# A hybrid decoder trunk: the first 60 microseconds with rows in groups of 128 tokens, x parts of two tiles per instruction, and low-part products last

## The chip, the cores and the metric

The kernel runs on one core of one Trainium2 chip. The metric is the device time of one execution in microseconds, lower is better. The profiler gives a second figure, the span from the first to the last recorded instruction of the core.

## What is computed

One inference step of a one-layer trunk over 2048 prompt tokens and 32 sample tokens (8 sequences of 4), 2080 tokens in all, with 1024 channels.

```
x = layer_norm(x, ln_in_g, ln_in_b)
proj = x @ w_in                       # 1024 -> 9 * 256 columns
xa, ga, xb, gb, gc, q, k, v, xp = jnp.split(proj, 9, axis=-1)
...                                   # four token mixers read proj: RG-LRU, short
...                                   # gated convolution, stick-breaking attention, pooling
out = jnp.concatenate([ya, yb, yc, yd], axis=-1) @ w_out
x = layer_norm(ALPHA * x + out, ln1_g, ln1_b)
x = layer_norm(ALPHA * x + jnp.square(jax.nn.relu(x @ w_ff1)) @ w_ff2, ln2_g, ln2_b)
```

Everything is float32. The change touches only the input layer norm and the first products of the input projection.

## The kernel before

**Blocks and tiles.** The 2080 tokens are five blocks (`NB`) of 416 tokens (`BLK`). The 1024 channels are eight tiles of 128 (`KT`), numbered k = 0 to 7. The 2304 columns of the input projection are 18 column tiles of 128, called p here in the order in which they are computed (`PORD`).

**Three products for one.** To keep float32 precision, each operand is split into a high part (rounded to the engine's fp32r format) and a low part (what is left). One block, one column tile and one channel tile cost three matmuls: w_hi·x_hi, w_hi·x_lo, w_lo·x_hi. A step is one (p, block) pair: 8 channel tiles, 24 matmuls of 416 columns into one PSUM bank. `P_STEPS` lists the steps: first the four column tiles p = 0 to 3 (`GRP`) for block 0, then for block 1, and so on to block 4; then the other column tiles. The text calls step j `project(j)`.

**The input layer norm.** Block b's rows come from memory with the tokens on the partitions, 104 tokens (`ROW`) in each of four groups (`NR`), each in two pieces of 96 and 8 rows (`ROW_PARTS`). They go to `rows_a` for even b and `rows_b` for odd b. VectorE (DVE) takes statistics (`block_var`: eight `bn_stats`, four `bn_aggr`, one add), ScalarE (ACT) takes the root (`block_std`), DVE the reciprocal (`block_nmr`), and then both engines normalise the rows in place: ACT group 0 and half of group 2, DVE the rest. TensorE (PE) transposes every channel tile back to channels-on-partitions (`turn_back(b, k)`: four transposes into PSUM bank 4 + k % 4). `block_back` finishes it: ACT (even k) or DVE (odd k) applies the layer norm's gain and bias while it moves the tile from PSUM to `x_full`; ACT makes x_hi by a copy; DVE makes x_lo by a subtraction. Every x tile goes through both engines.

**The weights.** `load_raw(p)` brings one column tile (128 x 1024 floats) into one of the two slots of `w_raw`. ACT makes the high part (`split_hi(p)`), DVE the low part (`split_lo(p)`); for p = 1 alone GpSimd (POOL) makes the low part.

**Order.** Each engine runs its own instructions in the order in which they are written, and waits on semaphores. Block 0's steps for p = 0 and 1 are computed together (`project_two`), so that each x tile is used as soon as it is there. ACT also copies each finished step out of PSUM (`put_out`). All these loads and stores are issued by SyncE (SP) on one queue, in program order. After block 4's first four column tiles (about 115 us) no line of the program differs any more.

Of the kernel before, what the change touches and what calls it, by code (L numbers as in the profile page):

```python
# [15 lines left out]
P = 128  # L16
# [62 lines left out]
ROW_PARTS = ((0, 96), (96, ROW))  # L79
NATB = NR * NB  # L80
# [167 lines left out]
def build(nc, x_all, w_all, pvec, lnp, rows2, gates_a, gates_x, poolw, sbh, sbr, masks, ident_d, ck, cv, ptab,  # L248
          st_h, st_a, st_b, st_p, y_out, kv_out, so_out):
    ctx = ExitStack()  # L250
    with ctx:
# [69 lines left out]
        with ExitStack() as e1:  # L321
            sb_at("x2_and_x3", [P, 2, 2, KT, BLK], F32, X_AT, e1)
# [103 lines left out]

        def raw_halves(n):

            return raw[:, n % 2, :].rearrange("p (k h c) -> p h k c", h=2, c=P)
# [8 lines left out]
        s_raw = [sem("raw_in0"), sem("raw_in1")]  # L438
        s_wh, s_wl = sem("w_hi_made"), sem("w_lo_made")
# [121 lines left out]
        def _(sp):  # L561
# [36 lines left out]
            load_rows(0)  # L598
            const(ident[:, :], ident_d)
# [238 lines left out]
        def _(pe):  # L838
            def turn_back(b, k):
# [6 lines left out]
                for j in range(NR):  # L846
                    ins = pe.transpose(PS[:, 4 + k % 4, j * ROW:(j + 1) * ROW], x_rows(b)[0:ROW, j, k * P:(k + 1) * P],
                                       ident[0:ROW, 0:ROW])
# [25 lines left out]
            def project_two():  # L874

                for k in range(KT):
                    pe.wait_ge(s_xl, k + 1)
                    for p in range(2):
                        if k == 0:
                            pe.wait_ge(s_wl, p + 1)  # L880
                        w_h, w_l = w_at(wp_hi(p), k), w_at(wp_lo(p), k)
                        out = PS[:, p, 0:BLK]
# [1716 lines left out]
```

## Time and profile before

| quantity | value |
|---|---|
| median of 3 executions | 2454.24 us (2453.53 to 2456.04) |
| profiled execution: its own time | 2453.47 us |
| profiled execution: span | 2451.9 us |
| TensorE matmul busy | 2410.5 us (98%) |
| VectorE busy | 1587.5 us (65%) |
| ScalarE busy | 1287.9 us (53%) |
| GpSimd busy | 242.4 us (10%) |

The profiled execution's own time lies 1.57 us above its span and 0.77 us below the median of the three. Busy time is time in which an engine works on an instruction; the idle time before an instruction is put down to whatever released it last. TensorE's matmuls are pipelined, so one matmul's printed duration (0.35 us) is longer than the distance from its start to the next one's (0.19 us): throughput is read from the starts.

### The profile page before, as it was taken

How to read it: one execution, taken by the hardware profiler on the slowest of the kernel's cores; microseconds unless marked ns; L12 is line 12 of the kernel's file. 1: busy time of each engine (PE TensorE's matmuls, PEld its weight loads, DVE VectorE, ACT ScalarE, POOL GpSimd, SP SyncE). 2: the span in 40 equal slices, each digit the busy share in tenths (PEclk: the TensorE clock that was granted, in tenths of full speed). 3: DMA queues.
4: the chain of work that ended last, by engine and by line, in shares of the span. 5: the costliest groups of instructions: out<-in, count | busy, mean ns of one | idle time of the engine just before them, and what ended most of it. 6: DMA issues, size and time to landing. Idle time of an engine off the chain costs nothing.

```text
span 2451.9 us, 36722 instructions
## 1 busy us (share of the span) xinstructions
PE 2410.5 (98%) x13263; PEld 2330.7 (95%) x13263; DVE 1587.5 (65%) x2234; ACT 1287.9 (53%) x1981; POOL 242.4 (10%) x526
## 2 busy tenths in 40 slices
PE   7999999999999999999999999999999999999998
PEld 7999999999999999999999999999999999999998
DVE  7535662656777787777778777757755665863335
ACT  5466523545656745556555566554445555444432
POOL 0011320200101100111100011000122130000000
PEclk9999999999999999999999999999999999999999
DMA  8434554533444434444443443433566674343332
GB/s 256 152 110 140 165 170 131 168 120 127 160 126 157 130 117 140 131 149 141 122 131 124 130 146 115 133 115 117 173 192 183 203 238 140 117 136 120 112 115 86
DMA packets 141526, 351.64 MB, mean 143 GB/s; under 512 B 20625, under 2 KB 64146, under 8 KB 141218
## 3 DMA queue, kind: packets, MB, share of 16 engines
q1 hardware_dynamic: 128994, 312.88, 40.2%
q0 software_dynamic: 12352, 36.42, 4.7%
q8 instruction: 106, 1.74, 0.3%
q14 instruction: 74, 0.61, 0.1%
HBM read 300.11 MB, written 49.12 MB: 142 GB/s over the span
## 4 chain that ended last, share of the span: by engine, by line
PE 92%; DVE 3%; ACT 2%; issue 1%; DMA 1%; SPq 0%; DVEq 0%; ACTq 0%
PE PS L1133 21%; PE PS L1135 21%; PE PS L1134 21%; PE PS L871 5%; PE PS L869 5%; PE PS L870 5%; PE PS L939 2%; PE PS L961 1%; PE PS L960 1%; PE PS L929 1%; PE PS L1023 1%; PE PS L930 1%; PE PS L1053 1%; PE PS L1011 1%; PE PS L909 1%
## 5 line engine op out<-in xcount | busy, mean ns | idle before, releaser
L1433 ACT ACTIVATE w_hi_lo<-w_raw 128x1024 fp32r<-128x1024 f32 x240 | 253.0, 1054 | 282.8 <-PE PS L1135 276.7
L1133 PE MATMUL PS<-a_hi,w_hi_lo 128*128 128x416 f32 x1080 | 385.0, 356 | 1.9 <-DVE a_lo L2185 1.9
L1135 PE MATMUL PS<-a_hi,w_hi_lo 128*128 128x416 f32 x1080 | 378.9, 351 | 0.0
L1134 PE MATMUL PS<-a_lo,w_hi_lo 128*128 128x416 f32 x1080 | 378.1, 350 | 0.0
L1986 DVE TENSOR_TENSOR w_hi_lo<-w_raw,w_hi_lo 128x1024 fp32r<-128x1024 f32 x240 | 292.7, 1220 | 57.2 <-ACT w_hi_lo L1433 54.9
L1133 PE MATMUL PS<-h_hi,w_hi_lo 128*128 128x416 f32 x824 | 294.3, 357 | 0.0
L1135 PE MATMUL PS<-h_hi,w_hi_lo 128*128 128x416 f32 x824 | 289.8, 352 | 0.0
L1134 PE MATMUL PS<-h_lo,w_hi_lo 128*128 128x416 f32 x824 | 288.9, 351 | 0.0
L2013 DVE TENSOR_TENSOR h_lo<-h_full,h_hi 128x416 fp32r<-128x416 f32 x160 | 94.6, 592 | 224.1 <-ACT h_hi L1448 223.9
L1133 PEld LDWEIGHTS PS<-a_hi,w_hi_lo 128*128 128x128 f32 x1080 | 202.8, 188 | 5.4 <-DVE a_lo L2185 2.8
L1134 PEld LDWEIGHTS PS<-a_lo,w_hi_lo 128*128 128x128 f32 x1080 | 203.3, 188 | 2.1
L1135 PEld LDWEIGHTS PS<-a_hi,w_hi_lo 128*128 128x128 f32 x1080 | 202.4, 187 | 2.3
L1433 ACT ACTIVATE w_hi_lo_c<-w_raw 128x1024 fp32r<-128x1024 f32 x120 | 126.5, 1054 | 132.8 <-PE PS L1135 128.4
L1444 ACT ACTIVATE h_full<-PS 128x416 f32<-128x416 f32 x160 | 82.5, 516 | 200.6 <-PE PS L1135 198.8
L1133 PE MATMUL PS<-a_hi,w_hi_lo_c 128*128 128x416 f32 x520 | 185.2, 356 | 2.2 <-DVE a_lo L2019 2.0
L1942 DVE TENSOR_TENSOR_SCAN n_prompt<-n_prompt 128x512 f32<-128x512 f32 (+3 forms) x160 | 178.9, 1118 | 8.6 <-POOL n_prompt L2508 8.4
L1135 PE MATMUL PS<-a_hi,w_hi_lo_c 128*128 128x416 f32 x520 | 183.2, 352 | 0.0
L1134 PE MATMUL PS<-a_lo,w_hi_lo_c 128*128 128x416 f32 x520 | 182.5, 351 | 0.0
L1986 DVE TENSOR_TENSOR w_hi_lo_c<-w_raw,w_hi_lo_c 128x1024 fp32r<-128x1024 f32 x120 | 146.3, 1220 | 34.1 <-ACT w_hi_lo_c L1433 33.2
L1134 PEld LDWEIGHTS PS<-h_lo,w_hi_lo 128*128 128x128 f32 x824 | 155.6, 189 | 2.1
L1133 PEld LDWEIGHTS PS<-h_hi,w_hi_lo 128*128 128x128 f32 x824 | 155.3, 188 | 2.2 <-issue 0.4
L1135 PEld LDWEIGHTS PS<-h_hi,w_hi_lo 128*128 128x128 f32 x824 | 154.8, 188 | 1.6
(334 smaller groups left out, 5206.4 us busy)
## 6 DMA issues: line engine op xcount, KB each, us to landing
w_raw<-w_all SPq DMA_DIRECT2D x380, 512.0 KB, 3.5
proj_scratch<-stage SPq DMA_DIRECT2D x70, 208.0 KB, 2.0
k_rows<-kv_out SPq DMA_DIRECT2D x80, 128.0 KB, 4.1
v_hi_lo<-v_scratch SPq DMA_DIRECT2D x40, 256.0 KB, 4.3
x_scratch<-x_full SPq DMA_DIRECT2D x20, 416.0 KB, 2.7
x_residual<-x_scratch SPq DMA_DIRECT2D x5, 1664.0 KB, 7.8
pages<-ck SPq DMA_DIRECT2D x64, 128.0 KB, 2.2
pages<-ck POOLq DMA_DIRECT2D x64, 128.0 KB, 2.6
```

What stands on the lines that cost most here:

```text
L869: pe.matmul(out, w_h, x_hi(b)[:, k, :], start=(k == 0), stop=False)
L870: pe.matmul(out, w_h, x_lo(b)[:, k, :], start=False, stop=False)
L871: ins = pe.matmul(out, w_l, x_hi(b)[:, k, :], start=False, stop=(k == KT - 1))
L939: ins = pe.transpose(PS[:, 5 + 2 * (t % 2), j * P:(j + 1) * P], sP[:, t % 3, j * P:(j + 1) * P], ident[:, :])
L1133: pe.matmul(out, w_h, mh_[:, k, :], start=(g == 0), stop=False)
L1134: pe.matmul(out, w_h, ml_[:, k, :], start=False, stop=False)
L1135: ins = pe.matmul(out, w_l, mh_[:, k, :], start=False, stop=(g == KT - 1))
L1433: act.activation(halves(w_hi(n)), raw_halves(n), ACT.Copy).then_inc(s_wh, 1)
L1444: act.activation(hf[:, f % 2, :], PS[:, (N_P + n) % 3, 0:BLK], ACT.Relu).then_inc(s_r, 1)
L1942: dve.tensor_tensor_scan(rev(n_t[:, 0:w]), rev(n_t[:, 0:w]), rev(n_t[:, 0:w]), n_t[:, w:w + 1], ALU.mult, ALU.bypass).then_inc(s_scan2, 1)
L1986: dve.tensor_tensor(halves(w_lo(n)), raw_halves(n), halves(w_hi(n)).bitcast(F32), ALU.subtract).then_inc(s_wl, 1)
L2013: dve.tensor_tensor(hl[:, i, :], hf[:, f % 2, :], hh[:, i, :].bitcast(F32), ALU.subtract).then_inc(s_hl, 1)
```

## The change

- **Rows.** A block's 416 tokens are cut into groups of 128, 128, 128 and 32 (`GROUPS`), each loaded by one transfer. SP waits until the second group of block 0 has landed before it issues anything else. The number of statistics, normalising and transpose instructions stays the same; their partition counts and widths change. `mv` is set to 1.0 beforehand, because the last group fills only 32 partitions.
- **Raw weights 2 and 3** get places of their own (in the idle tile `x2_and_x3`, called `x_and_x` in the rows), so their loads wait for nothing.
- **x parts.** ACT makes x_hi, and DVE x_lo, for two channel tiles (128 x 832) in one instruction. Each engine fills `x_full` for the next pair before it makes the parts of this pair.
- **Weight low parts.** DVE makes the low part for p = 1 too (POOL no longer), and `split_lo(0)`, `(1)`, `(2)` stand behind block 0's x parts. `split_hi(1)` stands behind x_hi of the first pair.
- **project_two** issues the two products with w_hi for all k first; the 16 products with w_lo follow as a group.
- **PE.** Four float32 matmuls on zeros stand ahead of everything (they wait for the second row group). `turn_back(1, 0..3)` moves from ahead of `project(3)` into its middle, `turn_back(1, 4..7)` from its middle to its end.

```diff
             def load_raw(p):
-                if p >= 2:
-                    sp.wait_ge(s_wl, p - 1)
+                if p in (2, 3):
+                    spare = x23[:, 1, p - 2, :, :].rearrange("p k t -> p (k t)")
+                    sp.dma_start(spare[:, 0:KT * P], w_all[AT[PORD[p]]]).then_inc(s_raw2[p - 2], 16)
+                    return
+                if p >= 4:
+                    sp.wait_ge(s_wl, p - 3 if p < 6 else p - 1)
...
-                for j in range(NR):
-                    at = b * BLK + j * ROW
-                    for first, last in ROW_PARTS:
-                        sp.dma_start(x_rows(b)[first:last, j, :], x_all[at + first:at + last]).then_inc(
-                            s_xin[b % 2] if b else s_xr0[j], 16)
+                for j, (first, last) in enumerate(GROUPS):
+                    sp.dma_start(x_rows(b)[0:last - first, j, :], x_all[b * BLK + first:b * BLK + last]).then_inc(
+                        s_xin[b % 2] if b else s_xr0[j], 16)
...
             load_rows(0)
+            sp.wait_ge(s_xr0[1], 16)
             const(ident[:, :], ident_d)
             const(ln_gb[:, :, :], lnp)
             load_raw(0)
             load_raw(1)
             load_rows(1)
             load_raw(2)
+            load_raw(3)
             for k in range(0, KT, 2):
                 store_x1(0, k)
-            load_raw(3)
...
                     for p in range(2):
                         if k == 0:
-                            pe.wait_ge(s_wl, p + 1)
+                            pe.wait_ge(s_wh, p + 1)
...
-                        ins = pe.matmul(out, w_l, x_hi(0)[:, k, :], start=False, stop=(k == KT - 1))
-                        if k == KT - 1:
-                            ins.then_inc(s_pst, 1)
-
+                for p in range(2):
+                    pe.wait_ge(s_wl, p + 1)
+                    for k in range(KT):
+                        ins = pe.matmul(PS[:, p, 0:BLK], w_at(wp_lo(p), k), x_hi(0)[:, k, :], start=False, stop=(k == KT - 1))
+                    ins.then_inc(s_pst, 1)
+
+            pe.wait_ge(s_zero, 1)
+            pe.wait_ge(s_xr0[1], 16)
+            for _ in range(4):
+                pe.matmul(PS[:, 7, 0:BLK], x23[:, 0, 0, 0, 0:P], x23[:, 0, 0, 0, :], start=True, stop=True)
...
+                    if b or p >= 2:
+                        project(b * GRP + p, turned=range(4) if b == 0 and p == 3 else ())
                     if b == 0 and p == 3:
-                        for k in range(4):
+                        for k in range(4, KT):
                             turn_back(1, k)
-                    if b or p >= 2:
-                        project(b * GRP + p, turned=range(4, KT) if b == 0 and p == 3 else ())
...
             def block_back(b, ks):                      # ACT
-                for k in ks:
-                    if k % 2 == 0:
...
-                    act.activation(x_hi(b)[:, k, :], x_full(b, k), ACT.Copy).then_inc(s_xh, 1)
+                whole(ks[0])
+                for k in ks[::2]:
+                    if k + 2 in ks:
+                        whole(k + 2)
+                    wait_apart(act, s_xfa, b * 4 + k // 2 + 1)
+                    act.wait_ge(s_xfd, b * 4 + k // 2 + 1)
+                    act.activation(x_hi(b)[:, k:k + 2, :], x_full(b, k, 2), ACT.Copy).then_inc(s_xh, 2)
+                    if b == 0 and k == 0:
+                        split_hi(1)
...
             def block_back(b, ks):                      # DVE
...
+                whole(ks[0] + 1)
+                for k in ks[::2]:
+                    if k + 2 in ks:
+                        whole(k + 3)
+                    dve.wait_ge(s_xh, b * KT + k + 2)
+                    dve.tensor_tensor(x_lo(b)[:, k:k + 2, :], x_full(b, k, 2), x_hi(b)[:, k:k + 2, :].bitcast(F32),
+                                      ALU.subtract).then_inc(s_xl, 2)
...
             dve.memset(gsel[:, :, :, :], 0.0).then_inc(s_mzero, 1)
+            dve.memset(x23[:, 0, 0, 0, :], 0.0).then_inc(s_zero, 1)
+            own.up(dve.memset(mv[:, :, :], 1.0))
             block_var(0)
             block_nmr(0)
-            split_lo(0)
             dve.wait_ge(s_const, 32)
             block_back(0, range(KT))
-            dve.wait_ge(s_wl, 2)
-            split_lo(2)
+            for p in range(3):
+                split_lo(p)
             block_var(1)
+            split_lo(3)
             block_nmr(1)
-            split_lo(3)
...
         def _(pool):
-            pool.wait_ge(s_wl, 1)
-            pool.wait_ge(s_wh, 2)
-            pool.tensor_tensor(halves(wp_lo(1)), raw_halves(1), halves(wp_hi(1)).bitcast(F32), ALU.subtract).then_inc(s_wl, 1)
```

DVE's instructions of the change's core, before: from the normalising of block 0's rows to the end of `split_lo(3)`. The left word is the line, then the operation, the written tile, the read tiles and the shape.

```order
L1722 TENSOR_SCALAR rows_a<-rows_a,rstd,nmr 104x1024 [waits nmr_made]
...
L1687 TENSOR_TENSOR w_hi_lo<-w_raw,w_hi_lo 128x2x512 [waits w_hi_made]
L1730 TENSOR_SCALAR x_full<-PS,ln_gb 128x416 [waits back_transposed,const_in]
L1734 TENSOR_TENSOR x_early<-x_full,x_early 128x416 [waits x_hi_made] x2
...
L1687 TENSOR_TENSOR w_hi_lo<-w_raw,w_hi_lo 128x2x512 [waits w_hi_made,w_lo_made]
L1697 BN_STATS bn<-rows_b 104x6 [waits xin_in_b]
L1697 BN_STATS bn<-rows_b 104x6 x7
...
L1722 TENSOR_SCALAR rows_b<-rows_b,rstd,nmr 104x1024
L1687 TENSOR_TENSOR w_hi_lo<-w_raw,w_hi_lo 128x2x512 [waits w_hi_made]
L1730 TENSOR_SCALAR x_full<-PS,ln_gb 128x416 [waits x_hi_made,x1_stored0,back_transposed]
```

The same stretch of DVE after the change:

```order
L1769 TENSOR_SCALAR x_full<-PS,ln_gb 128x416 [waits back_transposed,const_in]
L1769 TENSOR_SCALAR x_full<-PS,ln_gb 128x416 [waits back_transposed]
L1777 TENSOR_TENSOR x_early<-x_full,x_early 128x832 [waits x_hi_made]
...
L1777 TENSOR_TENSOR x_early<-x_full,x_early 128x832 [waits x_hi_made] x2
L1719 TENSOR_TENSOR w_hi_lo<-w_raw,w_hi_lo 128x2x512 [waits w_hi_made] x2
L1719 TENSOR_TENSOR w_hi_lo<-x_and_x,w_hi_lo 128x2x512 [waits w_hi_made]
L1733 BN_STATS bn<-rows_b 128x6 [waits xin_in_b]
L1733 BN_STATS bn<-rows_b 128x6 x5
L1733 BN_STATS bn<-rows_b 32x6 x2
...
L1719 TENSOR_TENSOR w_hi_lo<-x_and_x,w_hi_lo 128x2x512 [waits w_hi_made]
L1751 RECIPROCAL rstd<-std 128x4 [waits tile_normalised,std_made]
```

The first weight split has left its place ahead of block 0's x parts, three splits stand behind them, the fourth stands ahead of block 1's normalising instead of behind it, and eight single x_lo instructions have become four of 832 columns.

PE's instructions around the end of block 0, before (each row of L869 to L871 stands for one of 24 matmuls of a step):

```order
L871 MATMUL PS<-x_early,w_hi_lo 128x416
L847 MATMUL PS<-ident,rows_b 128x104 x16
L869 MATMUL PS<-x_early,w_hi_lo 128x416
...
L871 MATMUL PS<-x_early,w_hi_lo 128x416
L847 MATMUL PS<-ident,rows_b 128x104 x16
L869 MATMUL PS<-x_early,w_hi_lo 128x416
```

and after:

```order
L888 MATMUL PS<-x_early,w_hi_lo 128x416
L865 MATMUL PS<-ident,rows_b 128x128 x3
L865 MATMUL PS<-ident,rows_b 128x32
...
L886 MATMUL PS<-x_early,w_hi_lo 128x416
L887 MATMUL PS<-x_early,w_hi_lo 128x416
L888 MATMUL PS<-x_early,w_hi_lo 128x416
```

Before, the first 16 transposes of block 1 stand behind `project(2)` and the second 16 behind the first 12 matmuls of `project(3)`; after, the first 16 stand behind 36 matmuls (`project(2)` and half of `project(3)`) and the second 16 behind 12 more.

## Rows read from the trace of the kernel before

**Rows 1.** The page: busy us, share of the span and instructions of each engine.

```profile
PE 2410.5 (98%) x13263; PEld 2330.7 (95%) x13263; DVE 1587.5 (65%) x2234; ACT 1287.9 (53%) x1981; POOL 242.4 (10%) x526
```

**Rows 2.** A stage: us, busy PE, PEld, DVE, ACT, POOL, clock, DMA share, GB/s.

```profile
60.00:70.00 10.00, 10.00 (x63) 9.89 (x62) 8.32 (x14) 4.32 (x8) 0.00 (x0) 1.00 0.78 210
```

**Rows 3.** Timeline of PE: start us, us, line, what, count, idle before.

```profile
15.56 5.09 PE L847 MATMUL PS<-ident,rows_a 104*128 104x104 f32 x28 [15.56 <-ACT rows_a L1286]
21.73 0.96 PE L847 MATMUL PS<-ident,rows_a 104*128 104x104 f32 x4 [1.08 <-DVE x_full L1730]
...
22.88 0.55 PE L884 MATMUL PS<-x_early,w_hi_lo 128*128 128x416 f32 x1
...
24.96 0.45 PE L884 MATMUL PS<-x_early,w_hi_lo 128*128 128x416 f32 x1
25.25 0.35 PE L885 MATMUL PS<-x_early,w_hi_lo 128*128 128x416 f32 x1
...
32.78 0.35 PE L869 MATMUL PS<-x_early,w_hi_lo 128*128 128x416 f32 x1
...
37.31 1.59 PE L847 MATMUL PS<-ident,rows_b 104*128 104x104 f32 x16
38.68 0.43 PE L869 MATMUL PS<-x_early,w_hi_lo 128*128 128x416 f32 x1
...
54.30 1.62 PE L847 MATMUL PS<-ident,rows_a 104*128 104x104 f32 x16 [0.34 <-ACT rows_a L1286]
...
135.50 1.56 PE L909 MATMUL PS<-a_conv,gsel 128*128 128x416 f32 x4
```

**Rows 4.** Timeline of DVE, with the same columns.

```profile
4.77 1.29 DVE L1697 BATCH_NORM_STATS2 bn<-rows_a 104x6 f32<-104x512 f32 x2 [2.91 <-DMA rows_a<-x_all]
...
10.57 1.29 DVE L1697 BATCH_NORM_STATS2 bn<-rows_a 104x6 f32<-104x512 f32 x2 [0.26 <-DMA rows_a<-x_all]
...
13.43 1.99 DVE L1722 TENSOR_SCALAR rows_a<-rows_a,rstd,nmr 104x1024 f32<-104x1024 f32 x3
16.41 1.23 DVE L1687 TENSOR_TENSOR w_hi_lo<-w_raw,w_hi_lo 128x1024 fp32r<-128x1024 f32 x1 [0.99 <-ACT w_hi_lo L1271]
17.55 0.70 DVE L1730 TENSOR_SCALAR x_full<-PS,ln_gb 128x416 f32<-128x416 f32 x1
18.59 2.47 DVE L1734 TENSOR_TENSOR x_early<-x_full,x_early 128x416 fp32r<-128x416 f32 x2 [0.33 <-ACT x_early L1299]
...
23.52 1.20 DVE L1734 TENSOR_TENSOR x_early<-x_full,x_early 128x416 fp32r<-128x416 f32 x2
...
28.13 4.84 DVE L1697 BATCH_NORM_STATS2 bn<-rows_b 104x6 f32<-104x512 f32 x8
...
45.81 4.84 DVE L1697 BATCH_NORM_STATS2 bn<-rows_a 104x6 f32<-104x512 f32 x8
...
51.73 0.18 DVE L1715 RECIPROCAL rstd<-std 104x4 f32<-104x4 f32 x1 [0.27 <-ACT std L1279]
...
52.21 1.99 DVE L1722 TENSOR_SCALAR rows_a<-rows_a,rstd,nmr 104x1024 f32<-104x1024 f32 x3
```

**Rows 5.** Groups of one shape, 12 to 56 us: busy us, mean ns.

```profile
L1299 ACT ACTIVATE x_early<-x_full 128x416 fp32r<-128x416 f32 x16 | 8.6, 551 | 2.5 <-DVE x_full L1730 1.5
...
L1294 ACT ACTIVATE x_full<-PS,ln_gb 128x416 f32<-128x416 f32 x9 | 6.2, 687 | 0.3 <-PE PS L847 0.3
...
L1271 ACT ACTIVATE w_hi_lo<-w_raw 128x1024 fp32r<-128x1024 f32 x4 | 4.1, 1045 | 0.0
...
L2409 POOL TENSOR_TENSOR w_hi_lo<-w_raw,w_hi_lo 128x1024 fp32r<-128x1024 f32 x1 | 2.4, 2382 | 17.1 <-DVE w_hi_lo L1687 17.1
```

**Rows 6.** Single microseconds of the transfers: us, clock, DMA share, GB/s.

```profile
10.00:11.00 1.00, 1.00 1.02 387
11.00:12.00 1.00, 1.00 1.04 406
12.00:13.00 1.00, 1.00 1.06 246
```

More of the change, by code:

```diff
@@ L79 @@
 ROW_PARTS = ((0, 96), (96, ROW))
+GROUPS = [(a, min(a + P, BLK)) for a in range(0, BLK, P)]
 NATB = NR * NB
@@ L425, in halves, with raw_at, raw_in_halves @@
             return bass.AP(w[0], w[1] * HALF, [[WT, P], [ODD, 2], [P, KT // 2], [1, P]])
+        def raw_at(n):
+            return raw[:, n % 2, :]
+        def raw_in_halves(p):
+            if p not in (2, 3):
+                return raw_halves(p)
+            spare = x23[:, 1, p - 2, :, :].rearrange("p k t -> p (k t)")
+            return spare[:, 0:KT * P].rearrange("p (k h c) -> p h k c", h=2, c=P)
         def raw_halves(n):
-            return raw[:, n % 2, :].rearrange("p (k h c) -> p h k c", h=2, c=P)
+            return raw_at(n).rearrange("p (k h c) -> p h k c", h=2, c=P)
         def w_at(w, k):
@@ L845, in turn_back @@
                     pe.wait_ge(s_xfd if k % 2 else s_xfa, b * 4 + (k - 4) // 2 + 1)
-                for j in range(NR):
-                    ins = pe.transpose(PS[:, 4 + k % 4, j * ROW:(j + 1) * ROW], x_rows(b)[0:ROW, j, k * P:(k + 1) * P],
-                                       ident[0:ROW, 0:ROW])
+                for j, (first, last) in enumerate(GROUPS):
+                    n = last - first
+                    ins = pe.transpose(PS[:, 4 + k % 4, first:last], x_rows(b)[0:n, j, k * P:(k + 1) * P], ident[0:n, 0:n])
                 ins.then_inc(s_bt, 1)
@@ L1264, in split_hi @@
             def split_hi(p):
-                act.wait_ge(s_raw[p % 2], 16 * (p // 2 + 1))
+                if p in (2, 3):
+                    act.wait_ge(s_raw2[p - 2], 16)
+                else:
+                    act.wait_ge(s_raw[p % 2], 16 * max(p // 2, 1))
                 if p >= 4:
@@ L1278, in block_std @@
                 act.wait_ge(s_ve, b + 1)
-                act.activation(std[0:ROW, :], var[0:ROW, :], ACT.Sqrt).then_inc(s_std, 1)
+                act.activation(std[:, :], var[:, :], ACT.Sqrt).then_inc(s_std, 1)
             def block_norm(b):
@@ L1714, in block_nmr @@
                     dve.wait_ge(s_nat, NR * b)
-                own.up(dve.reciprocal(rstd[0:ROW, :], std[0:ROW, :]))
+                own.up(dve.reciprocal(rstd[:, :], std[:, :]))
                 own.sync()
-                dve.scalar_tensor_tensor(out=nmr[0:ROW, :], in0=mv[0:ROW, :, 0], scalar=-1.0, in1=rstd[0:ROW, :], op0=ALU.mult,
+                dve.scalar_tensor_tensor(out=nmr[:, :], in0=mv[:, :, 0], scalar=-1.0, in1=rstd[:, :], op0=ALU.mult,
                                          op1=ALU.mult).then_inc(s_nmr, 1)
@@ L1720, in block_nmr, with whole @@
                 for j, start in ((1, 0), (2, D // 2), (3, 0)):
-                    row = x_rows(b)[0:ROW, j, start:D]
-                    dve.tensor_scalar(row, row, rstd[0:ROW, j:j + 1], nmr[0:ROW, j:j + 1], ALU.mult, ALU.add).then_inc(s_natv, 1)
+                    row = x_rows(b)[0:size(j), j, start:D]
+                    dve.tensor_scalar(row, row, rstd[0:size(j), j:j + 1], nmr[0:size(j), j:j + 1], ALU.mult,
+                                      ALU.add).then_inc(s_natv, 1)
             def block_back(b, ks):
-                for k in ks:
-                    if k % 2:
-                        dve.wait_ge(s_bt, b * KT + k + 1)
-                        place_free(dve, s_xh, b, k)
-                        dve.tensor_scalar(x_full(b, k), PS[:, 4 + k % 4, 0:BLK], ln_gb[:, 0, k:k + 1], ln_gb[:, 1, k:k + 1],
-                                          ALU.mult, ALU.add).then_inc(s_xfd, 1)
-                        for d in (k - 1, k):
-                            dve.wait_ge(s_xh, b * KT + d + 1)
-                            dve.tensor_tensor(x_lo(b)[:, d, :], x_full(b, d), x_hi(b)[:, d, :].bitcast(F32), ALU.subtract).then_inc(s_xl, 1)
+                def whole(k):
+                    dve.wait_ge(s_bt, b * KT + k + 1)
+                    place_free(dve, s_xh, b, k)
+                    if b == NB - 1 and k >= 4:
+                        dve.wait_ge(s_xl, b * KT + k - 3)
+                    dve.tensor_scalar(x_full(b, k), PS[:, 4 + k % 4, 0:BLK], ln_gb[:, 0, k:k + 1], ln_gb[:, 1, k:k + 1],
+                                      ALU.mult, ALU.add).then_inc(s_xfd, 1)
```

47 lines of the change are left out of this document (25 added, 22 removed).

## The prediction, made before the changed kernel ran

> **What bounds the kernel now.** I read the busy time by engine first: PE is busy in 2410.5 of 2451.9 us [rows 1]. The stages then show where it is not: from 60 us on it is busy in 10.00 of 10 [rows 2], and the lines of the change end at about 115 us. So only the start can give something, and a microsecond won there is a microsecond of the whole, if nothing takes it back. The timeline of PE shows what there is to win [rows 3]: PE waits until 15.56 us for block 0's normalised rows, again 1.08 us before the last four transposes, and once more at 54.30 us for block 2's rows (0.34 us by the row). A 416-column matmul follows the one before at 0.35 us between 22.88 and 24.96 (six in 2.08 us: 1.2 GHz), and at 0.188 us from 25.25 to 32.78 (40 of them: the 2.4 GHz level). The granted clock in the stage rows says 1.00 throughout, so here I trust the starts.
>
> The timeline of DVE shows who makes PE wait [rows 4]. The row groups land one after another, the first at 4.77 and the last at 10.57 us, and everything up to 15.42 us (13.43 + 1.99) is a chain behind the last one. From 37 us to 54.20 us DVE works almost without a pause, and its normalising of block 2 (52.21 + 1.99 = 54.20) is what PE waits for at 54.30. **That is the point I calculate to**: from block 2's transposes on, PE has no further wait, so the kernel ends earlier by what those transposes start earlier than 54.30. PE may be far ahead in between; it must wait there for DVE.
>
> **Rows in 128-token groups.** The transfer rate is 246 GB/s while rows go (12 to 13 us), and 387 and 406 GB/s while the two raw weight tiles pass (10 to 12 us, mean 396) [rows 6]. Those have 128 partitions of 4 KB, exactly the form of the new groups; the rows before go in pieces of 96 and 8. At 396 GB/s a group of 524 KB takes 1.3 us, against 426 KB at 246 GB/s, 1.7 us. The first lands at 4.77 - 0.4 = 4.4 us, the next at 5.7, 7.0 and (32 rows) 7.4. Two statistics instructions take 1.2 us (8 in 4.84 [rows 4]), so DVE hardly waits: the third pair starts at 7.05 and all is done 2.45 later, at 9.5 us, against 10.57 + 1.29 = 11.86. **Gain 2.35 us**, and block 0's normalising ends at 13.1 us instead of 15.42. Holding back the later loads costs nothing: raw weight 0 is issued near 7 us and needed at 13.1, which covers more than twice its own 1.3 us; the two memsets on DVE (the nearest row, 128x768 zeros, is not longer than DVE's 2.91 us wait for the first rows) lie ahead of the first rows.
>
> By the Trainium skill (page "DMA: Bandwidth & Descriptors", section "Why a DMA increments its semaphore by 16 and not by 1") a transfer uses the largest number of engines, at most 16, that divides its partition count: 96 partitions run on 16 engines, 8 on 8. By that rule the busiest engine has 7 rows of an old group and 8 of a new one, and the old form would not be slow; the rate in the rows says that it is. This is a rival below.
>
> **DVE's chain from there, step by step.** Starts of neighbours lie a little closer than their durations, so I use distances between starts. Prices: x_full 0.70 (0.65 to the next), weight low part 1.15 (16.41 to 17.55), statistics up to the variance 5.6 (45.81 to 51.46, where the 0.27 us of waiting for the root begin), reciprocal to the end of normalising 2.47 (51.73 to 54.20) [rows 4]. ACT: x_full 0.69, weight high part 1.0 [rows 5]. The pair of 832 columns is in no row. It lies between 416 and 1024 columns: on ACT 0.55 and 1.05, on DVE 0.60 (half of 1.20) and 1.23 [rows 4, 5]; by the length I take 0.9 and 1.02. The bounds, 1.05 and 1.23 per pair above and half of that below, move a block by at most 0.8 us. One tile's four transposes take 0.343 us at the upper level (16 in 1.37, 37.31 to 38.68), 0.73 at the lower one (28 in 5.09) [rows 3].
>
> *PE's clock.* The four float32 matmuls on zeros start near 5.7. Four of that shape take 1.56 us at the upper level [rows 3] (L909, 135.50), so about 3 at the lower one: they end near 8.8, and PE idles until 13.2. Before, 28 transposes in 5.09 us did not raise the clock, so I take the lower level for block 0's transposes, and the upper one some us later, as before.
>
> *Block 0.* Transposes from 13.2: tile 1 is there at 14.9 and tile 3 at 16.3. x_full of 1 ends at 15.6, of 3 at 17.0. ACT has done weight 0 (14.0), x_full of 0 and, behind tile 2, of 2 (16.3), and the first x_hi pair at 17.1. x_lo pair and x_full of 5 to 18.8; wait 0.75, since ACT puts the high part of weight 1 in between (pair 2 at 19.5). Three more x_lo pairs with x_full of 7: 23.1. Three weight low parts, 3.45: 26.6.
> *Block 1's rows.* Statistics 5.6: 32.2. Weight 3, 1.15: 33.35. Reciprocal to normalised, 2.47: 35.8. PE transposes at 35.9 (before 37.31).
> *Block 1's x.* x_full of 1 and 3 until 38.2, first pair of x_hi at 38.8, x_lo pair until 39.8. Then a new wait: tiles 4 and 5 are transposed only behind four tiles (1.37) and 12 matmuls (2.26), from 39.55, and are there at 40.5. x_full of 5, x_hi pair at 41.7, three pairs of x_lo with x_full of 7: 45.25.
> *Block 2.* From the statistics' start to the transposes 8.49 (45.81 to 54.30): **53.7 us instead of 54.30, a gain of 0.6 us**.
>
> So the way from block 0's rows to block 2's is 1.7 us longer than before (40.5 against 38.8), though two things on it get cheaper. POOL's weight low part (2.38 us [rows 5]) is gone, beside which two x_lo instructions took 2.47 instead of 1.20 us [rows 4]: 1.27 saved. Four pairs instead of eight singles save 4 x 0.18 us in each of the blocks 0 and 1, together 1.4. Against that stand 1.15 for the fourth weight low part on DVE, the waits of 0.75 and 0.7 above, 0.5 to 0.6 at each first pair, that the first x_full pair now waits for transposes at the lower level (about 1.0; before, a weight split filled that time), and that the last weight part now stands ahead of block 1's normalising (1.15, of which 0.8 had been waited anyway).
>
> **PE's part.** project_two can begin near 18.8; its 48 matmuls, 9.0 us at 0.188 and about 1 us more at first, end near 29, some 4 us before the 32.78 of before. But that lead is given back by waits behind it: for the fourth weight low part (33.4) before project(3), for x_lo in block 1's first step, and about 2.7 us before block 2's transposes. Issuing the w_lo products last is therefore worth nothing at the end, and the zero matmuls, which lie in a wait, cost nothing.
>
> **The sum.** Span 2451.9 - 0.6 = 2451.3, the profiled execution 2453.47 - 0.6 = 2452.9. The median of the runs lies 0.77 above that execution: 2454.24 - 0.6 = **2453.6 us**. 0.2% of the time, about what a measurement can tell from no change, is 4.9 us.
>
> **Rivals.**
> 1. *The rows come no faster.* The 246 GB/s belong to the source, not to the form. Then a group takes 2.1 us: landings at 5.2, 7.3 and 9.3, statistics done at 11.75 (gain 0.1 instead of 2.35), and with the 1.7 from above the kernel is **1.6 us slower**. Against it stand the 387 and 406 of [rows 6], seen with the same partitions and row length. The skill's rule above gives nearly this: 8/7 of the mean landing distance ((10.57 - 4.77)/3 = 1.93) is 2.2 us. Chance 0.18.
> 2. *The clock is up from block 0 on.* The zero matmuls raise it and it stays up. A tile's transposes then take 0.343 instead of 0.73, x_full of 1 starts at 14.1 and all behind it is 1.0 earlier: **gain 1.6 us**. Against it, 5.09 us of transposes did not raise it, and the zeros are shorter and followed by 4.4 us of nothing. Chance 0.16.
> 3. *The other side: the clock falls in the new wait.* PE now waits some 2.7 us before block 2's transposes, where it waited 0.34. A way back from the low level is in the rows: 21.73 to 24.96 us, four transposes at +0.09 each and eight matmuls at +0.16, 1.6 us lost [rows 3]; the whole low stretch from 15.56 would be 4.7 us. With one such return the kernel is 1.0, with the long one **4.1 us slower**; it turns slower once the low stretch exceeds 1.2 us. For it speaks that PE was at the low level at 22 us after a pause of 1.08; against it, that PE had then never been at the upper one. Chance 0.10. The Trainium skill (page "TensorE: Matmul & The Clock Gate", section "HAM oscillation") says that matmul bursts with long waits between them fall back to half rate each time.
> 4. *The lead is kept.* If DVE's chain is shorter than I have it (pairs near the lower bound, no waits), PE keeps its 4 us or more: **gain 3 to 5.6 us**. Against it: DVE has 39 us of work in a row there. Chance 0.08.
>
> **How the numbers follow.** The forecast has 0.43 (0.2 slower to 1.3 faster), the rivals 0.52, the rest 0.05. The number is the forecast's, 2453.6. The range leaves out the far parts of rivals 3 and 4 (each by half) and little else: gain 4.2 to 2.6 slower, 2450.0 to 2456.8, which also takes in that three executions of one kernel lay 2.5 us apart. Faster by over 4.9 us is only the far end of rival 4: 0.03. Slower by as much needs rivals 1 and 3 at once: 0.02. Within 0.2%: 0.95.
>
> **What would show it.** Row landings: the second pair of statistics follows the first with hardly a wait, the last ends near 9.5. Chain: block 0's transposes near 13.2, project(2) near 29, project(3) waiting for the fourth weight low part until 33.4, block 2's transposes near 53.7 with an idle time of about 2.7 before them, none behind 60 us. Clock: transposes of one tile 0.73 apart at 13 us, 0.35 between matmuls at first, 0.188 soon after. Wrong would be: statistics still paced by landings; tiles 0.34 apart at 13 us; 0.35 between matmuls behind 53 us; or no wait at all before block 2.

## The result and the profile after

| | before | after |
|---|---|---|
| median | 2453.91 us (2453.53 to 2456.04) | 2471.14 us (2470.61 to 2473.34, 4 executions) |
| ratio after to before | | 1.0069, 95% interval 1.0057 to 1.0082 |
| profiled execution, span | 2453.47, 2451.9 us | 2471.05, 2469.3 us |

The kernel is 17 us slower, and the interval leaves no room for no change. The page's first row, as in [rows 1], shows on which engine: PE is busy 22.7 us longer with eight more records, while DVE and ACT have hardly changed. So PE's own instructions take longer.

```profile
PE 2433.2 (99%) x13271; PEld 2340.4 (95%) x13271; DVE 1584.8 (64%) x2217; ACT 1285.4 (52%) x1961; POOL 243.5 (10%) x525
```

The timeline of PE after, the counterpart of [rows 3] (start us, us, line, what, count, idle before):

```profile
5.98 4.88 PE L910 MATMUL PS<-x_and_x 128*128 128x416 f32 x8 [5.98 <-DMA rows_a<-x_all]
14.02 8.63 PE L865 MATMUL PS<-ident,rows_a 128*128 128x128 f32 x32 [3.16 <-ACT rows_a L1311]
22.58 0.71 PE L899 MATMUL PS<-x_early,w_hi_lo 128*128 128x416 f32 x1
...
30.63 3.19 PE L904 MATMUL PS<-x_early,w_hi_lo 128*128 128x416 f32 x16
...
40.48 2.62 PE L865 MATMUL PS<-ident,rows_b 128*128 128x128 f32 x16
43.03 0.46 PE L886 MATMUL PS<-x_early,w_hi_lo 128*128 128x416 f32 x1
...
86.23 2.62 PE L865 MATMUL PS<-ident,rows_b 128*128 128x128 f32 x16
88.78 0.46 PE L886 MATMUL PS<-x_late,w_hi_lo 128*128 128x416 f32 x1
...
151.21 1.56 PE L931 MATMUL PS<-a_conv,gsel 128*128 128x416 f32 x4
```

Sixteen transposes in a row are four tiles; the text calls them a burst. Before, a burst took 1.37 us up to the next matmul (37.31 to 38.68 in [rows 3]); now it takes 2.55 (86.23 to 88.78), though PE waits for no other engine there. That is 0.30 us more per tile, at every one of the 24 tiles of blocks 2 to 4, where each microsecond of PE counts. The last row is the first matmul of the later gates (L909 in [rows 3]). It comes at 151.21 instead of 135.50 us, 15.7 later, and what follows it takes 2318.1 us against 2316.4, which is within the 2316 to 2320 of the other traces. **I call this start the gate mark below.** The only two traces of one kernel (E7 and E14) had it at 134.20 and 134.69. Executions of one kernel lie 2.5 us and more apart in the whole time, so the mark seems the sharper measure, though each kernel has it from one trace.

PE's weight loads at 86 us name the place inside a tile:

```profile
86.04 0.44 PEld L865 LDWEIGHTS PS<-ident,rows_b 128*128 128x128 f32 x3
86.64 0.48 PEld L865 LDWEIGHTS PS<-ident,rows_b 32*128 32x128 f32 x4 [0.17 <-issue]
87.30 0.48 PEld L865 LDWEIGHTS PS<-ident,rows_b 32*128 32x128 f32 x4 [0.17 <-issue]
```

Each row of four is one 32-row load and the three 128-row loads of the next tile, 0.65 us from row to row. Before each 32-row load the loader stands still for 0.17 us though the profile shows nothing that it awaits (`issue`). Before the change all 16 loads stand in one row without idle time:

```profile
37.12 1.57 PEld L847 LDWEIGHTS PS<-ident,rows_b 104*128 104x128 f32 x16
```

DVE after, the counterpart of [rows 4]:

```profile
4.66 2.50 DVE L1733 BATCH_NORM_STATS2 bn<-rows_a 128x6 f32<-128x512 f32 x4 [2.33 <-DMA rows_a<-x_all]
7.88 2.46 DVE L1733 BATCH_NORM_STATS2 bn<-rows_a 128x6 f32<-128x512 f32 x4 [0.72 <-DMA rows_a<-x_all]
...
11.89 1.98 DVE L1758 TENSOR_SCALAR rows_a<-rows_a,rstd,nmr 128x1024 f32<-128x1024 f32 x3
16.32 0.71 DVE L1769 TENSOR_SCALAR x_full<-PS,ln_gb 128x416 f32<-128x416 f32 x1 [2.44 <-PE PS L865]
18.39 0.71 DVE L1769 TENSOR_SCALAR x_full<-PS,ln_gb 128x416 f32<-128x416 f32 x1 [1.36 <-PE PS L865]
...
41.84 0.71 DVE L1769 TENSOR_SCALAR x_full<-PS,ln_gb 128x416 f32<-128x416 f32 x1 [3.90 <-PE PS L865]
...
57.74 1.98 DVE L1758 TENSOR_SCALAR rows_a<-rows_a,rstd,nmr 128x1024 f32<-128x1024 f32 x3
```

The rows do land sooner: statistics end at 10.34 (7.88 + 2.46), not at 11.86. But now DVE waits for PE's transposes (2.44, 1.36, 3.90 us), and block 2's normalising ends at 59.72 (57.74 + 1.98) instead of 54.20. The stages (us, busy PE, PEld, DVE, ACT, POOL, clock, DMA share, GB/s) add the clock:

```profile
12.00:14.00 2.00, 0.00 (x0) 0.01 (x1) 1.87 (x3) 2.00 (x3) 0.00 (x0) 0.78 1.00 410
14.00:26.00 12.00, 11.98 (x42) 8.69 (x43) 7.22 (x9) 9.34 (x12) 0.00 (x0) 0.50 0.78 277
...
56.00:60.00 4.00, 1.65 (x10) 1.31 (x9) 3.10 (x11) 2.41 (x4) 0.00 (x0) 1.00 0.70 255
60.00:62.00 2.00, 2.00 (x11) 1.23 (x10) 0.71 (x1) 0.84 (x2) 0.00 (x0) 0.73 0.31 111
62.00:66.00 4.00, 4.00 (x14) 3.42 (x14) 1.64 (x2) 2.38 (x3) 0.00 (x0) 0.50 0.51 197
```

The granted clock is at 0.50 (1.2 GHz) in block 0, and again from 61 to 67 us, behind the wait ahead of block 2 (PE busy 1.65 of 4 us).

### The profile page after: what moved, and what is told of

It reads as the page before. It is cut to its first block, busy times and chain, and to the rows that moved or that the text cites. A ratio compares the mean times of both kernels' runs of the same rounds, so it can differ in the third digit from the quotient of the medians.

```text
span 2469.3 us, 36723 instructions
## 1 busy us (share of the span) xinstructions
PE 2433.2 (99%) x13271; PEld 2340.4 (95%) x13271; DVE 1584.8 (64%) x2217; ACT 1285.4 (52%) x1961; POOL 243.5 (10%) x525
## 4 chain that ended last, share of the span: by engine, by line
PE 93%; DVE 3%; ACT 2%; issue 1%; DMA 0%; DVEq 0%; ACTq 0%; SPq 0%
PE PS L1155 21%; PE PS L1157 21%; PE PS L1156 21%; PE PS L886 5%; PE PS L888 5%; PE PS L887 5%; PE PS L961 2%; PE PS L983 1%; PE PS L982 1%; PE PS L951 1%; PE PS L1045 1%; PE PS L952 1%; PE PS L1075 1%; PE PS L1033 1%; PE PS L865 1%
```

## The experiments

"Theory A" in the expectations is that the step in height (the rows of the weight) between a 128-row and a 32-row transpose costs 0.30 us per tile. All kernels compute the whole of the reference. Where no other kernel is named, ratios are to the kernel before, run on the same chip in the same turn.

**E1: the kernel before, with the changed groups alone.**

```diff
+GROUPS = [(a, min(a + P, BLK)) for a in range(0, BLK, P)]   # 128, 128, 128, 32
...
-                for j in range(NR):
-                    ins = pe.transpose(PS[:, 4 + k % 4, j * ROW:(j + 1) * ROW], x_rows(b)[0:ROW, j, k * P:(k + 1) * P],
-                                       ident[0:ROW, 0:ROW])
+                for j, (first, last) in enumerate(GROUPS):
+                    n = last - first
+                    ins = pe.transpose(PS[:, 4 + k % 4, first:last], x_rows(b)[0:n, j, k * P:(k + 1) * P], ident[0:n, 0:n])
```

> The kernel before with one part of the change alone: rows in groups of 128, 128, 128 and 32 tokens. Theory A (the step between a 128-row and a 32-row weight in PE's transposes costs time): a tile's four transposes start 0.65 us after the last tile's instead of 0.34, 40 tiles give 12 us, so 2463 to 2468 us. Theory B (the loss comes from the moved waits and the clock they cost, and a tile is slow only where PE waits): within 2 us of 2454, tiles 0.34 to 0.36 us apart. Theory C (any transpose of 128 rows and columns is slow): as A, but the time lies in the 128-row ones, which would start 0.18 us apart.

Measured: 2464.71 us, ratio 1.0041 (1.0026 to 1.0055), gate mark 146.12: as theory A had it. The groups alone cost 10.6 us at the gate mark, although block 0's transposes begin at 14.34, 1.2 us sooner than before. Block 2's begin 3.4 us later (57.70 against 54.30), and six bursts of 1.2 us more are the rest. The burst at 81 us:

```profile
81.14 2.62 PE L847 MATMUL PS<-ident,rows_b 128*128 128x128 f32 x16
83.69 0.46 PE L868 MATMUL PS<-x_late,w_hi_lo 128*128 128x416 f32 x1
```

**E2: the changed kernel with four groups of 104 again**, each one transfer.

```diff
-GROUPS = [(a, min(a + P, BLK)) for a in range(0, BLK, P)]
+GROUPS = [(a, a + ROW) for a in range(0, BLK, ROW)]
```

> The changed kernel with four groups of 104 rows again, each in one transfer. Theory A: all tiles 0.34 us apart, the wait before block 2 is back to under 2 us, 2451 to 2456 us. Theory B: the reordered waits remain, so 2464 to 2470 us.

**E3: the changed kernel, its last transpose made over 128 rows**, of which 96 are zeros.

```diff
-                    n = last - first
+                    n, last = P, first + P
...
+            for t in (rows_a, rows_b):
+                pool.memset(t[:, NR - 1, :], 0.0).then_inc(s_pad, 1)
```

> The changed kernel with the last group's transposes made 128 rows tall and 128 columns wide (96 of the rows are zeros that are written once at the start, their columns are not read). Theory A: no step in height is left, a tile takes 0.44 us (512 columns in two passes), 40 x 0.21 = 8.4 us and some of the follow-up are won, 2457 to 2463 us. Theory C: 128-row transposes are slow themselves, a tile takes 0.7 us or more, 2472 us or more. Theory B: no difference from the changed kernel, 2470 to 2472 us.

Measured: E2 2458.40 us, ratio 1.0016 (1.0006 to 1.0025), gate mark 137.67; E3 2457.40 us, 1.0012 (1.0003 to 1.0022), gate mark 138.27. Taking the 32-row transposes away, in two ways, takes 13.5 and 12.9 us of the 15.7 off. E3 keeps the count of transposes and the quick transfers and even transposes more columns, so neither the count nor the bytes cost. Theory A had E2 at 2451 to 2456 us, so it was missed by 2.4: some 2 to 3 us are left. In E2 they are a late start, block 2's transposes beginning at 56.46 instead of 54.30. In E3 those begin at 53.69, 0.6 sooner than before; its padded bursts cost 0.3 each (6.28 from one to the next where it was 5.98 before), 1.8 in six; and block 2's two bursts are 7.86 apart and not 6.28, 1.6 us. Together these give 138.3, the mark that E3 has. The last part is the clock, in single microseconds around block 2's start:

```profile
53.00:54.00 1.00, 0.31 (x2) 0.34 (x3) 0.59 (x1) 1.00 (x2) 0.00 (x0) 0.72 0.00 0
54.00:55.00 1.00, 1.00 (x7) 1.00 (x6) 0.00 (x0) 0.20 (x2) 0.00 (x0) 0.50 0.22 60
```

In block 0, however, E3's clock stayed up, unlike the changed kernel's, and 32 transposes took 3.69 us:

```profile
13.51 3.69 PE L868 MATMUL PS<-ident,rows_a 128*128 128x128 f32 x32 [3.01 <-ACT rows_a L1314]
```

```profile
14.00:16.00 2.00, 2.00 (x21) 2.00 (x20) 1.23 (x2) 1.89 (x4) 0.00 (x0) 1.00 1.08 383
```

**E4: E2 with block 1's `turn_back` where it was before the change.**

```diff
-                        project(b * GRP + p, turned=range(4) if b == 0 and p == 3 else ())
                     if b == 0 and p == 3:
-                        for k in range(4, KT):
+                        for k in range(4):
                             turn_back(1, k)
+                    if b or p >= 2:
+                        project(b * GRP + p, turned=range(4, KT) if b == 0 and p == 3 else ())
```

> As the one with 104-row groups, and block 1's transposes back in their old places (four tiles ahead of project(3), four in its middle). My ledger has 0.7 us of DVE waiting for tiles 4 and 5 and, on the other side, PE waiting for block 1's rows ahead of project(3): 0 to 1.5 us faster than with the new places. Rival: the new places keep PE dense, and the old ones cost 1 us or more.

Measured: 2459.32 us, 1.0021 (1.0011 to 1.0030), gate mark 141.44. With the old places PE waits for block 1's rows instead, 2.85 us, and the clock falls there:

```profile
39.40 3.01 PE L865 MATMUL PS<-ident,rows_b 104*128 104x104 f32 x16 [2.85 <-ACT rows_b L1311]
```

The mark is 3.8 us later than E2's, so the rival of the expectation came out and not the 0 to 1.5 us gain. The new places of `turn_back` are therefore no cost of the change; whether they gain is not told by the whole times, whose intervals overlap.

**E5 and E6: the fourth group as a plain float32 matmul over 128 rows**, of 32 columns, in the changed kernel (E5) and the kernel before with the new groups (E6).

```diff
+                    ins = pe.matmul(PS[:, 4 + k % 4, first:last], x_rows(b)[:, j, k * P:(k + 1) * P], ident[:, 0:last - first],
+                                    start=True, stop=True, is_transpose=True if j < NR - 1 else None)
```

> The changed kernel with all weights of the transposes 128 rows tall and the old 416 columns: the last group's rows 32 to 127 are zeros written once, and its 32 columns come from a plain float32 matmul with the identity's first 32 columns. Theory A (the step in height costs the time): tiles 0.35 us apart, 2.9 us less than with the padded 512 columns, block 2's transposes near 53.5: 2453.5 to 2456 us. Rival (any change between neighbours costs, the change from transpose to plain matmul as well): tiles 0.5 us or more, 2457 to 2462 us.

> The kernel before with the 128-token row groups and the same even heights, nothing else of the change. Theory A: tiles 0.35 us apart. The transposes of block 0 start near 14.3, 1.2 us earlier than before, but before block 2 PE is held by its own work (it waited 0.34 there), so 0 to 0.8 us faster than before: 2453.5 to 2454.5 us. Rival (the 128-token groups bring 1.2 us or more by themselves): under 2453.2 us.

Measured: 2461.74 us, 1.0028 (1.0017 to 1.0040), gate mark 140.89, and 2456.63 us, 1.0011 (1.0001 to 1.0020), gate mark 137.44. Both lie above what theory A had (2453.5 to 2456 and 2453.5 to 2454.5); E5 came out as its rival. The weight height is even now, and the price halves but isn't gone. In E6 it is (76.77 - 74.79)/4 = 0.50 us per tile. Besides the height, two things differ from the transposes of before: a plain matmul stands between transposes, and its 32 columns are fewer than its neighbours'. No run tells which of them, or the second record, makes the 0.15 us that remain. In E6 block 2's transposes begin at 52.55, 1.75 us sooner than before, and six bursts of 0.6 us more take it back. The count of 20 in the row shows that the plain float32 matmul is recorded twice.

```profile
74.79 2.14 PE L849 MATMUL PS<-ident,rows_b 128*128 128x128 f32 x20
76.77 0.44 PE L871 MATMUL PS<-x_late,w_hi_lo 128*128 128x416 f32 x1
```

**E7 and E8: other uneven groups in the kernel before.** E7 has 112, 112, 96, 96 tokens, E8 112, 104, 100, 100, in single transfers (one execution each). The edit is E1's with

```diff
+GROUPS = [(0, 112), (112, 224), (224, 320), (320, 416)]     # E7
+GROUPS = [(0, 112), (112, 216), (216, 316), (316, 416)]     # E8
```

> The kernel before with row groups of 112, 112, 96 and 96. It asks what kind of step costs: if a change of the number of 32-row strips (four for 112, three for 96) does, tiles are 0.55 to 0.65 us apart; if only a step from 128 down to 32 rows does, 0.35.

> The kernel before with row groups of 112, 104, 100 and 100: heights differ, all take four strips of 32 rows. If the number of strips counts, tiles are 0.35 us apart; if any change of height does, 0.6 us or more.

Measured: 2454.14 us with the gate mark at 134.20, and 2456.09 us at 136.82. Steps of 4 to 16 rows cost nothing: 1.38 us per burst in E7, and 1.40 in E8. E8 starts late, at 17.30 us, and its mark is late; a second trace of it, which could tell whether that is its groups or chance, was not taken.

```profile
73.95 1.60 PE L847 MATMUL PS<-ident,rows_b 112*128 112x112 f32 x16
75.33 0.43 PE L868 MATMUL PS<-x_late,w_hi_lo 128*128 128x416 f32 x1
```

**E9 to E12: the remaining 2 to 3 us.** E9 is the changed kernel with E7's groups; E10 is E9 with three more matmuls on zeros in the wait ahead of block 2; E11 is E9 without the four matmuls on zeros at the start; E12 is E7 with those four (the lines that E11 drops).

```diff
+GROUPS = [(0, 112), (112, 224), (224, 320), (320, 416)]     # all four
...
+                    if b == 1 and p == 2:                       # E10
+                        pe.wait_ge(s_xfd, 8)
+                        for _ in range(3):
+                            pe.matmul(PS[:, 7, 0:BLK], x23[:, 0, 0, 0, 0:P], x23[:, 0, 0, 0, :], start=True, stop=True)
...
-            for _ in range(4):                                  # E11
-                pe.matmul(PS[:, 7, 0:BLK], x23[:, 0, 0, 0, 0:P], x23[:, 0, 0, 0, :], start=True, stop=True)
```

> The changed kernel with row groups of 112, 112, 96 and 96 tokens, everything else as changed. Theory A (only the step to a 32-row weight costs): a tile's four transposes take 0.35 us as in the strip of 112/112/96/96 in the kernel before, block 1's and 2's bursts 1.4 us each; and since no transfer is as quick as the 128-partition one, block 0's transposes start near 14.0 to 14.8, block 2's at 53.0 to 54.5, and the first gate matmul at 133.5 to 135.5 us; time 2452 to 2456. Rival (something else of the change costs the remaining 2 to 3 us, for example w_lo products last or the places of turn_back): bursts are 1.4 us and the first gate matmul still comes at 137 to 138.5.

> As the kernel before it in this call, and three float32 matmuls on zeros ahead of block 2's first transposes, in the idle time there. Theory C (the clock falls in that new wait): without them block 2's first 16 transposes take 3.2 us with the granted clock at 0.5, with them 1.4 to 1.6 at 1.00, and the first gate matmul comes 1.0 to 1.7 us sooner. Rival: the clock does not fall in the wait without them (bursts are 1.4 us in both), and the two are the same within 0.3 us.

> The changed kernel with groups of 112, 112, 96 and 96 and without the four float32 matmuls on zeros at the start. If they raise the clock for block 0: without them block 0's tiles are 0.73 us apart instead of 0.35 and the first matmuls 0.35 apart, all behind it 1.0 to 1.6 us later until DVE's chain absorbs it, first gate matmul 0.5 to 1.6 us later. If they do nothing (my prediction's cost of zero): within 0.3 us.

> The kernel before with groups of 112, 112, 96 and 96 and with the four float32 matmuls on zeros, nothing else of the change. If theory A and the account of the clock hold: block 0's tiles 0.35 us apart, block 0's transposes at 14.8, block 2's near 52 to 52.9, first gate matmul at 133.0 to 134.2, 1.3 to 2.5 us sooner than the kernel before: time 2451.5 to 2453. Rival: it comes as the strip alone did (134.2), because DVE's chain and not the transposes pace block 0.

| | median us | ratio (interval) | block 0 | block 2 | gate mark |
|---|---|---|---|---|---|
| E9 | 2457.35 | 1.0012 (1.0002 to 1.0021) | 14.40 | 55.08 | 137.99 |
| E10 | 2456.23 | 1.0005 (0.9995 to 1.0015) | 14.29 | 54.96 | 136.29 |
| E11 | 2456.73 | 1.0007 (0.9997 to 1.0017) | 15.04 | 55.71 | 138.69 |
| E12 | 2453.99 | 0.9996 (0.9987 to 1.0006) | 14.76 | 53.45 | 134.78 |

(Block 0 and block 2 are the starts of their first transposes.) E9's bursts are back at 1.61 us by their rows (E7: 1.60), and its mark missed the expected 133.5 to 135.5: the rival, that something else of the change costs 2 to 3 us, is right. A part of it is in the comparison with E10. Ahead of block 2, E9 waits and then takes 3.01 us for its burst; with the wait filled the same burst takes 1.63:

```profile
55.08 3.01 PE L865 MATMUL PS<-ident,rows_a 112*128 112x112 f32 x16 [2.38 <-ACT rows_a L1312]
62.68 1.61 PE L865 MATMUL PS<-ident,rows_a 112*128 112x112 f32 x16
```

```profile
52.42 2.26 PE L920 MATMUL PS<-x_and_x 128*128 128x416 f32 x6
54.96 1.63 PE L865 MATMUL PS<-ident,rows_a 112*128 112x112 f32 x16 [0.28 <-ACT rows_a L1316]
61.00 1.61 PE L865 MATMUL PS<-ident,rows_a 112*128 112x112 f32 x16
```

The second burst comes 6.04 us behind the first with the fill and 7.60 without, 1.6 us, and the mark is 1.7 sooner, as expected: the fall of the clock, which the stages (as above; E9 first) show in E9 and not in E10:

```profile
56.00:58.00 2.00, 2.00 (x14) 2.00 (x13) 0.71 (x1) 1.26 (x2) 0.00 (x0) 0.50 0.33 111
```

```profile
56.00:58.00 2.00, 2.00 (x16) 1.99 (x15) 1.47 (x3) 1.97 (x4) 0.00 (x0) 1.00 0.49 186
```

That is one trace of each kernel, and the whole times, whose intervals overlap, don't resolve it. Behind much the same wait (2.35 to 2.39 us) the clock also fell in the changed kernel, E3, E11 and E13, but not in E2 and E5, which have no fill. So the fall costs what the rows say, but that the fill prevents it in every execution isn't shown. The other 0.8 us of E9's 2.5 are its start of block 2, 55.08 instead of 54.30.

The matmuls on zeros at the start do nothing at the mark that can be told from the spread: E11 without them is 0.7 us later at the mark, but began 0.6 later; E12 with them is at 134.78 (133.0 to 134.2 was expected), where E7 and E14 without are at 134.20 and 134.69. In block 0 itself 32 transposes take 5.78 us with them (E9) and 4.82 without (E11), so they didn't speed those up.

**E13: the changed kernel, the 32-row transposes of four tiles put together** (blocks 1 to 4).

```diff
+                for k in four:
+                    pe.wait_ge(s_xfd if k % 2 else s_xfa, b * 4 + (k - 4) // 2 + 1)
+                    for j in range(3):
+                        pe.transpose(PS[:, 4 + k % 4, j * P:(j + 1) * P], x_rows(b)[:, j, k * P:(k + 1) * P], ident[:, :])
+                for k in four:
+                    pe.transpose(PS[:, 4 + k % 4, 3 * P:BLK], x_rows(b)[0:32, 3, k * P:(k + 1) * P], ident[0:32, 0:32]).then_inc(s_bt, 1)
```

> The changed kernel; only the order of the transposes of blocks 1 to 4 differs: in each burst of four tiles the twelve 128-row transposes come first and the four 32-row ones behind them, so that there are two steps in weight height per burst and not eight. If it is the step that costs (0.30 us per tile, one pair of steps): each of the eight bursts takes 1.6 to 1.8 us instead of 2.62, and the first gate matmul comes some 6 to 8 us sooner than the 151.2 of the changed kernel, at 143 to 145.5; time 2463 to 2465. Rival (it is the 32-row transpose itself that is slow, 0.3 us each wherever it stands): bursts stay at 2.6, first gate matmul at 150 to 152, time as the changed kernel, 2471.

Measured: 2463.57 us, 1.0039 (1.0023 to 1.0054), gate mark 143.74, 7.5 us sooner than the changed kernel, as expected if the step costs. The weight loads at 82 us:

```profile
81.73 1.42 PEld L876 LDWEIGHTS PS<-ident,rows_b 128*128 128x128 f32 x12
83.31 0.32 PEld L878 LDWEIGHTS PS<-ident,rows_b 32*128 32x128 f32 x4 [0.17 <-issue]
83.67 0.19 PEld L898 LDWEIGHTS PS<-x_late,w_hi_lo 128*128 128x128 f32 x1
```

The same 16 transposes, in another order, pause once (0.17 us) instead of four times, and the four 32-row loads take 0.32 us together. So it is the change, there and back, that costs, and not the small transpose. The small transposes differ from the others in rows and in columns at once. E5 and E6, which even out the rows, take away half of the price, so the height has a share; how much of the other half is the columns' stays open.

**E14: E7 again, timed**, since its mark was the earliest.

> The kernel before with row groups of 112, 112, 96 and 96 tokens in single transfers, whose first gate matmul stood at 134.2 instead of 135.5 us in one look: 1.3 us sooner, so 2453 against 2454.4, ratio 0.9990 to 1.0000. Rival: what comes sooner there is lost behind 135 us in the spread of the later work, and no difference can be measured.

Measured: 2453.92 us, ratio 1.0000 (0.9991 to 1.0009), gate mark 134.69. The 0.8 to 1.3 us at the mark can't be told in the whole time. No version here beats the kernel before by more than its measurement can tell.

## Why the prediction was wrong

**The step that failed** is the price of a tile's transposes: "One tile's four transposes take 0.343 us at the upper level (16 in 1.37, 37.31 to 38.68), 0.73 at the lower one (28 in 5.09)". I took it from rows of the 104-row form and used it for 128, 128, 128 and 32, though it is the one PE instruction whose form the change alters, and it does so in every block. I had bounded the pair of 832 columns, which no row showed either, but not this. It measured 0.64 us at the upper level (2.55/4) and 1.07 at the lower (8.56/8, 14.02 to 22.58). The extra was about the same at either clock level (0.30 and 0.34). I had read [rows 2] only as saying that nothing can be won behind 60 us; PE is the limit there, so it also says that a dearer PE instruction is paid in full.

**The ledger of the miss.** I expected the gate mark at 135.50 - 0.6 = 134.9; it came at 151.2, 16.3 later.
- Rows: block 0 starts at 14.02 and not 13.2, 0.8 us.
- Up to block 2: from 14.02 to 59.82 are 45.8 us against my 40.5, so 5.3. Up to block 1's transposes it is 26.5 (to 40.48) against 22.7 (13.2 to 35.9), so 3.8: eight tiles of block 0 at 0.34 more are 2.7, and project_two, whose first twelve matmuls are 0.35 apart, takes 11.1 (22.58 to 33.65) instead of 10.2, 0.9. PE's path is now the longer one: DVE has block 1's rows done at 37.94 and then waits 3.90 for PE. From there to block 2's transposes it is 19.3 instead of 17.8, 1.5 of the 2.4 that block 1's eight tiles add at 0.30 each; the rest lies beside other work.
- Transposes from block 2 on: six bursts at 1.18 more (2.55 against 1.37), 7.1 us.
- Clock behind block 2's wait: its two bursts start 10.16 us apart (59.82 to 69.98), where 6.02 + 1.18 = 7.2 were due, 3.0 us.

Together 16.2. E1, E2, E3 and E13 show the second and third. For the fourth, E9 and E10 show 1.6 us; why the low stretch was longer in the changed kernel (61 to 67.7 us, against 55 to 58.3 in E9) no run shows.

**Point by point.**
- *The rows land faster* (gain 2.35): right in kind, 1.5 in size (10.34 instead of 9.5). The third group came later than I had it, DVE waiting 0.72 for it. Rival 1 fell.
- *DVE's chain*: 40.5 us from block 0's transposes to block 2's, predicted. Without the 32-row step it took 39.8 (E2), 40.2 (E3) and 40.7 (E9, E10, E11), against 38.7 before. This part held, with the wait of about 2.4 at its end. E9's wait for the fourth weight low part (0.38, at 34.57) was there too.
- *The matmuls on zeros* cost nothing: right, but they took 4.88 us and not "near 3". Four are issued and eight recorded, and the row of four from which I priced them is two matmuls as well (`a_gates` issues two).
- *The clock in block 0*: low, as taken, in the changed kernel (0.50 from 14 to 26 us), so rival 2 is not what happened there. It did happen in E3 (1.00 throughout, 0.46 us per padded tile), behind a pause of 3.01 us, longer than E9's of 2.73, where the clock fell; so the length of the pause alone doesn't tell.
- *Rival 3, the clock falls in the new wait* (0.10; 1.0 to 4.1 us): it happened, 3.0 us in the changed kernel, 1.5 to 1.6 in E3, E9, E11 and E13, and alone it would have turned the sign. I gave it too little: the wait came as calculated (2.4 us for 2.7). It isn't certain each time: E2 and E5, with waits of 2.39 and 2.35 us, kept the clock at 1.00.
- *Rival 4*, the lead is kept: the changed kernel never had it, since project(2) began at 33.65 us (before: 32.78, forecast: 29). E9 had it (29.48), and gave it back, as forecast.
- *No idle time behind 60 us* was right too, and it didn't help.

Two versions show what the change is without the step. E3 keeps its 128-row transfers: block 2 begins at 53.69 where I had 53.7, but partly by luck, since its clock was up in block 0, which I had priced at 1.0 us, and its transposes were padded. In E9 and E10, with 112 and 96 rows that land later, block 2 begins 0.7 to 0.8 us later than before. In E3 and E9 the clock's fall then adds 1.6. None of them is faster than before.

Before the change the weight loads run ahead of the transposes: the first starts at 37.12 us, the first transpose at 37.31. The Trainium skill (page "TensorE: Matmul & The Clock Gate", section "Step-by-step: what each phase is for") says that a load is pulled ahead when the row groups don't conflict or when it goes to the background weight buffer, and also that the weight's row count doesn't matter for its timing. The second sentence fits 104, 112, 100 and 96 rows here; with 128 next to 32 the trace has 0.17 us of standstill ahead of the 32-row load. That a conflict of row groups is the mechanism is a reading that no run here tests: the trace shows only that standstill, and it is about half of the 0.30 us.

## What to carry to other kernels

When a change alters the shape of an instruction that the bounding engine runs everywhere, price that shape apart, and bound it upwards too, even if count and bytes stay the same. Keep neighbouring transposes at like heights (four of 104, or 112 and 96) instead of filling 128 and leaving a rest of 32; where a small rest can't be avoided, put the rests of several tiles together. A wait of 2.4 us ahead of matmuls costs more than itself when the clock falls in it or just behind it (1.6 and 3.0 us here); in the one pair of traces that compares it, three matmuls on zeros that fill the wait brought 1.6 us back.

## What the runs showed of the hardware

- A pair of steps between 128-row and 32-row transposes costs 0.30 us at the upper clock level (E1, and the changed kernel) and 0.34 at the lower; steps of 4 to 16 rows cost nothing (E7 and E8: 1.38 and 1.40 us per burst). Putting four rests together brought a burst from 2.55 to about 1.75 us (81.92 to 83.67).
- A plain float32 matmul of 32 columns among transposes, at even height, costs too: 0.50 instead of 0.35 us per tile (E6), its second record included.
- Single transfers of 104 rows were not quicker than the pieces of 96 and 8, whose first and last pairs of statistics start at 4.77 and 10.57 us [rows 4], 1.93 us per group. In E2 the statistics pairs start at 5.45, 7.45, 9.46 and 11.65 us, and in E3, with groups of 128, the third pair starts at 7.36 and all are done at 9.82. The rule of the Trainium skill that I had weighed (page "DMA: Bandwidth & Descriptors", section "Why a DMA increments its semaphore by 16 and not by 1": the largest divisor up to 16) gives, worked out, eight rows per engine for both, 104 on 13 and 128 on 16. My estimate from it would be no difference in the time of a group; the runs show one of 0.6 us (2.0 against 1.4).
- In the changed kernel the records of the matmuls on zeros start 0.69 us apart from 6.81 to 9.58 us, and the last two, at 10.00 and 10.35, are 0.35 apart: the clock rose to the upper level (2.4 GHz) during them. PE then had nothing to do for 3.2 us, and the granted clock of block 0's transposes was 0.50 (1.2 GHz) again. In E3, behind a pause of 3.0 us, it was 1.00.
